# Moving the rounds of a top-k search on VectorE: the first token half's rounds go beside the indexer, the second half's go one to every two attention units

## The chip, the cores and the metric

The kernel runs on one core of one Trainium2 chip. The metric is the device time of one execution in microseconds (us), lower is better. The engines are named as in the profile: PE (TensorE matmul), PEld (its weight loads), DVE (VectorE), ACT (ScalarE), POOL (GpSimd), SP (the queue that issues the DMAs).

## The reference, cut to what matters

The program is one dense transformer block and then two layers of a second kind, for 256 tokens. Each of the two layers mixes tokens with two attentions of 8 heads, and one of them sees only keys that an indexer has chosen:

```python
n_keep = min(TOPK_MAX, T // 4)                     # 64 of 256 keys
rel = relu(einsum('bthd,bsd->bths', iqb, ik) * IDX_DIM ** -0.5)   # 8 indexer heads
score = einsum('bths,bth->bts', rel, iwb)
score = where(key_idx <= tq, score, -inf)
_, sel = top_k(score, n_keep)                      # the sparse attention (DSA) reads these keys
# the first attention (MLA) needs none of it
s = einsum('bthd,bshd->bhts', qb, k) * scale
p = softmax(where(key_idx <= tq, s, -inf))
```

Everything is float32. After the two attentions come an output projection, a layer norm, a router and 16 experts.

## The kernel before, in words

The kernel is one program in which every engine has its own instruction stream, written in the order in which it runs; semaphores join them. There is no scheduler. The 256 tokens are two halves of 128 (`half` 0 and 1); because of causality half 0 has 128 keys and half 1 has 256.

In each of the two layers these stages follow one another:

1. The indexer, 16 steps `i` (`half`, head): PE makes a score tile (L2347) between the matmuls of three projections (L2054 to L2056), ACT applies the relu into one of two `logit` buffers (L1018), DVE adds it, weighted, to `score` (`idx_add`, L1753 and L1756; the profile calls this tile `bias_h`). PE's tile of step i waits for relu i-2, relu i waits for add i-2, so the three run at most two steps apart. DVE also copies projection results out of PSUM (`save_half`, L1309) after steps 6, 10 and 14. POOL turns the queries by their positions meanwhile (`rotate`, L662 to L665).
2. The turning of q and k: PE transposes pairs of heads (L1979) into four banks used in turn. ACT copies q out (L1047), DVE copies k out (L1786, `k_t`). Group i of k is only written once the copy of group i-2 is done, and DVE's copies stand behind all 16 adds. Then PE makes sums for the router (L2385).
3. The first attention, 16 units (half, head): PE scores (L2133), DVE adds the mask and takes the row maximum (`logits`, L1279), ACT takes the exponential (`exps`, L839), PE transposes (L1979), ACT copies (L848) and casts a quarter slab of the next weights (L755), PE weighs the values (L2149). `attention` on DVE takes `before` and `after`, called around each unit's `logits`. After unit 12 DVE divides and saves the first half (`save(0)`, L1285 and L1288), at the end the second.
4. The sparse attention, whose `logits` first adds the selection to a bias (L1272).

The largest 64 keys of a row are found in 8 rounds for each half. A round is `largest(i)`, which takes the 8 largest (MAX, L1802), and `take(i)`, which overwrites them (MATCH_REPLACE, L1807, two instructions in the trace). `selection()` then turns what was taken into a mask (L1816, L1821). Before the change all 16 rounds stand in the first attention, one to a unit, round i around unit i.

Of the kernel before, what the change touches and what calls it, by code (L numbers as in the profile page):

```python
# [30 lines left out]
ALU = mybir.AluOpType  # L31
AX = mybir.AxisListType

P = 128
SEQ, D = 256, 1024
HALVES = SEQ // P
DC = D // P
HEADS, HD = 8, 64
WIDTH = HEADS * HD
EPS_RMS, EPS_LN = 1e-6, 1e-5  # L40
NEG = -1e30
# [15 lines left out]
IDX_HEADS, IDX_D = 8, 32  # L57
KEEP = SEQ // 4
# [22 lines left out]
SC_MLA = MLA_D ** -0.5  # L81
# [3 lines left out]
TAKEN = -3e38  # L85
# [14 lines left out]
L_IN, L_IN_B, L_IN_C, L_QUP, L_UK, L_UV, L_O = 0, 4, 6, 7, 9, 10, 11  # L100
# [144 lines left out]
def build(nc, A, out):  # L245

    ctx = ExitStack()
    with ctx:
        def sb(name, shape, dt=F32):
            return ctx.enter_context(nc.sbuf_tensor(name, shape, dt))  # L250

        S = {name: ctx.enter_context(nc.semaphore(name)) for name in SEMAPHORES}
        bank = [ctx.enter_context(nc.psum_tensor(f"bank{i}", [P, 512], F32)) for i in range(8)]
# [21 lines left out]
        value = sb("value", [P, HALVES, WIDTH])  # L275
# [3 lines left out]
        k_t = sb("k_t", [P, HEADS, SEQ])  # L279
# [38 lines left out]
        mask = const[:, C_MASK:C_DIST].rearrange("p (a t) -> p a t", a=HALVES)  # L318
        dist = const[:, C_DIST:C_COS1].rearrange("p (a t) -> p a t", a=HALVES)
        before, one = marks[:, 0:P], marks[:, P:P + 1]  # L320
# [21 lines left out]
        k_up = wide_b[:].rearrange("p (a h d) -> p a h d", a=HALVES, h=HEADS)  # L342
# [94 lines left out]
        def wait_slab(eng, name, n, j=None, per=0):  # L437

            eng.wait_ge(S[name], count(n + 1, j, per))
# [34 lines left out]
        IDX_AFTER_QUP, IDX_AFTER_UK, IDX_AFTER_UV = 6, 10, 14  # L474
        N_IDX = HALVES * IDX_HEADS
# [22 lines left out]
        def k_turned(i):  # L498
            return bank[3 - 2 * (i % 2)]
# [700 lines left out]
        def _(dve):  # L1200
            w = Waits(dve, S)
            split = [0]
            tt = nc.vector.tensor_tensor
# [102 lines left out]
            def save_half(n, name, saves):  # L1306
                wait_slab(dve, "slab_used", n)
                for dst, src in saves:
                    nc.vector.tensor_copy(dst, src).then_inc(S[name], 1)  # L1309
# [305 lines left out]
            for g in range(GROUPS):  # L1615
                nc.vector.scalar_tensor_tensor(
                    out=xs[:, 4 + g, SEQ:2 * SEQ], in0=bank[6 + g // 2][:, (g % 2) * SEQ:(g % 2 + 1) * SEQ],
                    scalar=vec[:, V_PS + g:V_PS + g + 1], in1=xs[:, 4 + g, 0:SEQ].bitcast(F32),
                    op0=ALU.mult, op1=ALU.subtract).then_inc(S["mixed_lo"], 1)
# [38 lines left out]
            for i in range(HALVES):  # L1658
# [7 lines left out]
                                               scalar=1.0 / D, in1=stat[:, 1, 4 + i:5 + i], op0=ALU.mult,  # L1666
                                               op1=ALU.add).then_inc(S["mean_square"], 1)
# [47 lines left out]
            for layer in range(LAYERS):  # L1715
                b = layer_base(layer)
# [27 lines left out]
                score = sel_score  # L1744

                def idx_add(i):
                    half, h = divmod(i, IDX_HEADS)
                    keys = P * (half + 1)
                    dst = score[:, half, 0:keys]
                    w.next("idx_relu")  # L1750
                    weight = idx_w[:, half, h:h + 1]
                    if h == 0:
                        nc.vector.tensor_scalar(dst, logit[:, i % 2, 0:keys], weight, None, ALU.mult)\  # L1753
                            .then_inc(S["idx_added"], 1)
                    else:
                        nc.vector.scalar_tensor_tensor(out=dst, in0=logit[:, i % 2, 0:keys], scalar=weight, in1=dst,  # L1756
                                                       op0=ALU.mult, op1=ALU.add).then_inc(S["idx_added"], 1)
                    w.next("idx_added")

                def save_qup(i):  # L1760
                    save_half(b + L_QUP + i, "qup_saved1",
                              [(q_up[:, 1, 4 * i:4 * i + 4, 0:MLA_D],
                                bank[QUP_BANKS[i] + 1][:, 0:4 * MLA_D].rearrange("p (h d) -> p h d", h=4))])
# [8 lines left out]
                turned_b(5)  # L1772
                splits_to(b + L_UV)
                w.next("idx_masked")
                for i in range(N_IDX):
                    idx_add(i)
                    if i + 1 == IDX_AFTER_QUP:
                        save_qup(1)
                    if i + 1 == IDX_AFTER_UK:
                        save_half(b + L_UK, "kv_saved1",  # L1780
                                  [(k_up[:, 1, :, 0:HD], bank[1][:].rearrange("p (h d) -> p h d", h=HEADS))])
                    if i + 1 == IDX_AFTER_UV:
                        save_half(b + L_UV, "kv_saved1", [(value[:, 1, :], bank[5][:])])
                for i in range(4):
                    w.next("turned_a", 2)
                    nc.vector.tensor_copy(k_t[:, 2 * i:2 * i + 2, :], k_turned(i)[:].rearrange("p (c t) -> p c t", c=2))\  # L1786
                        .then_inc(S["copied_k"], 1)
                for half in range(HALVES):
                    keys = P * (half + 1)
                    dst = score[:, half, 0:keys]  # L1790
                    tt(dst, dst, mask[:, half, 0:keys], ALU.add).then_inc(S["idx_masked"], 1)
                w.next("idx_masked", HALVES)

                assert KEEP // 8 == HEADS

                def largest(i):
                    half = i // HEADS
                    if i:  # L1800
                        w.next("vector_step")
                    nc.vector.max(best, score[:, half, 0:P * (half + 1)]).then_inc(S["vector_step"], 1)  # L1802

                def take(i):
                    dst = score[:, i // HEADS, 0:P * (i // HEADS + 1)]
                    w.next("vector_step")
                    nc.vector.match_replace(dst, best, dst, TAKEN).then_inc(S["vector_step"], 1)  # L1807

                def selection():

                    w.next("vector_step")
                    for half in range(HALVES):
                        keys = P * (half + 1)
                        dst = score[:, half, 0:keys]

                        nc.vector.tensor_scalar(dst, dst, TAKEN * 0.5, -NEG, ALU.is_le, ALU.mult).then_inc(S["vector_step"], 1)  # L1816
                    w.next("vector_step", HALVES)
                    for half in range(HALVES):
                        keys = P * (half + 1)
                        dst = score[:, half, 0:keys]  # L1820
                        nc.vector.scalar_tensor_tensor(out=dst, in0=dst, scalar=NEG, in1=mask[:, half, 0:keys],  # L1821
                                                       op0=ALU.add, op1=ALU.add).then_inc(S["vector_step"], 1)
                    w.next("vector_step", HALVES)

                attention(SC_MLA, 0, before=largest, after=take, at_end=selection)

                def heads_low(i):

# [872 lines left out]
```

## Time and profile before

| | us |
|---|---|
| median of 3 runs | 1126.9 (1126.75 to 1127.37) |
| the profiled execution | 1127.47 |
| its span, first to last instruction | 1125.7 |
| PE busy | 1076.1 (96%) |
| DVE busy | 563.8 (50%) |
| ACT busy | 436.8 (39%) |

The span holds two layers of the second kind; the indexer of the first begins near 428 us and its first attention near 447 us, those of the second near 801 and 820 us. DVE's 50% is a mean over stages: between 463 and 467 us it is nearly fully busy.

### The profile page before, as it was taken

The page shows a single profiled execution, that of the slowest core. Times are in us where ns is not written, and L with a number is a line of the kernel's source. Part 1 is how long each engine was busy: PE and PEld are TensorE (multiplying, and loading weights), DVE is VectorE, ACT ScalarE, POOL GpSimd, SP SyncE. Part 2 cuts the span into 40 slices and gives each one's busy share as a digit, 9 for nine tenths or more (in the row PEclk, how much of TensorE's full clock was granted, in tenths as well). Part 3 has the DMA queues.
Part 4 walks back from the last instruction along what each step waited for, and adds up shares of the span by engine and source line. Part 5 has one row for each costly group of instructions (what it writes and reads, how often), then busy time and mean ns, then how long its engine had stood idle before and what let it go on. Part 6 is the DMA issues. An engine that isn't in the chain of part 4 may idle for free.

```text
span 1125.7 us, 16190 instructions
## 1 busy us (share of the span) xinstructions
PE 1076.1 (96%) x6206; PEld 741.4 (66%) x6210; DVE 563.8 (50%) x1081; ACT 436.8 (39%) x797; POOL 90.0 (8%) x113
## 2 busy tenths in 40 slices
PE   8999998999999999899999999989989999999996
PEld 5898987999999788686444443348977744444332
DVE  4664376676676647846422222264685642232224
ACT  5445455554554435744211111144475422221111
POOL 1200000000000011520000000020242000000000
PEclk8999998999999999899999999989989999999998
DMA  7843245545655345428999999944542989999993
GB/s 273 269 145 130 89 150 185 179 162 189 202 166 189 128 147 184 152 98 357 411 420 422 419 422 422 419 176 151 187 144 82 376 355 422 420 421 420 422 420 144
DMA packets 82829, 294.60 MB, mean 262 GB/s; under 512 B 8424, under 2 KB 41542, under 8 KB 58058
## 3 DMA queue, kind: packets, MB, share of 16 engines
q1 hardware_dynamic: 79888, 289.33, 67.5%
q10 hardware_dynamic: 2874, 4.36, 1.0%
q8 instruction: 44, 0.72, 0.3%
q14 instruction: 23, 0.19, 0.0%
HBM read 292.62 MB, written 1.05 MB: 261 GB/s over the span
## 4 chain that ended last, share of the span: by engine, by line
PE 82%; DVE 6%; DMA 6%; ACT 3%; issue 2%; SPq 0%; DVEq 0%; POOL 0%; ACTq 0%
PE bank L2519 16%; PE bank L2528 9%; PE bank L2054 8%; PE bank L2055 8%; PE bank L2056 8%; DMA early_w<-in_w_up 5%; PE bank L2115 4%; PE bank L2117 4%; PE bank L2116 4%; PE bank L1979 4%; PE bank L2506 3%; PE bank L2149 3%; PE bank L2551 2%; PE bank L2133 2%; PE bank L2231 1%
## 5 line engine op out<-in xcount | busy, mean ns | idle before, releaser
L1208 DVE TENSOR_TENSOR lo<-raw,hi 128x2048 fp32r<-128x2048 f32 (+3 forms) x77 | 164.7, 2146 | 63.8 <-ACT hi L747 63.5
L747 ACT CAST hi<-raw 128x2048 fp32r<-128x2048 f32 (+3 forms) x78 | 139.5, 1795 | 60.9 <-PE bank L2056 58.6
L1454 DVE TENSOR_TENSOR proj<-bank,proj 64x512 f32<-64x512 f32 x32 | 34.7, 1083 | 210.0 <-PE bank L2541 209.9
L2115 PE MATMUL bank<-xs,hi 128*128 128x256 f32 x448 | 128.8, 287 | 3.1 <-DVE xs L1238 1.5
L2054 PE MATMUL bank<-hi,xs 128*128 128x512 f32 (+2 forms) x312 | 125.3, 402 | 6.6 <-DVE xs L1242 3.4
L2116 PE MATMUL bank<-xs,hi 128*128 128x256 f32 x448 | 127.7, 285 | 0.0
L2117 PE MATMUL bank<-xs,lo 128*128 128x256 f32 x448 | 127.7, 285 | 0.0
L2056 PE MATMUL bank<-lo,xs 128*128 128x512 f32 (+2 forms) x312 | 118.6, 380 | 0.0
L2055 PE MATMUL bank<-hi,xs 128*128 128x512 f32 (+2 forms) x312 | 118.5, 380 | 0.0
L1137 ACT ACTIVATE proj<-bank 64x512 f32<-64x512 f32 x32 | 18.9, 589 | 191.4 <-PE bank L2520 191.4
L2115 PEld LDWEIGHTS bank<-xs,hi 128*128 128x128 f32 x448 | 87.0, 194 | 4.6 <-issue 3.0
L2116 PEld LDWEIGHTS bank<-xs,hi 128*128 128x128 f32 x448 | 87.0, 194 | 0.4
L2117 PEld LDWEIGHTS bank<-xs,lo 128*128 128x128 f32 x448 | 86.9, 194 | 0.0
L2054 PEld LDWEIGHTS bank<-hi,xs 128*128 128x128 f32 x312 | 60.1, 193 | 16.8 <-DVE lo L1553 3.7
L2520 PE MATMUL bank<-moe_w,xg 128*64 128x512 f32 x160 | 70.3, 592 | 0.0
L1472 DVE SCALAR_TENSOR_TENSOR expert_out<-bank,slot_gate,expert_out 128x512 fp32r<-128x512 f32 x32 | 24.0, 751 | 88.8 <-ACT expert_out L1150 88.8
L2056 PEld LDWEIGHTS bank<-lo,xs 128*128 128x128 f32 x312 | 59.8, 192 | 10.7
L2055 PEld LDWEIGHTS bank<-hi,xs 128*128 128x128 f32 x312 | 60.2, 193 | 8.9
L1150 ACT ACTIVATE expert_out<-bank,slot_gate 128x512 fp32r<-128x512 f32 x32 | 22.0, 688 | 110.8 <-PE bank L2528 110.8
L1689 DVE SCALAR_TENSOR_TENSOR proj<-bank,conv,proj 128x255 f32<-128x255 f32 (+1 forms) x88 | 38.5, 478 | 48.7 <-ACT proj L967 45.8
L2528 PE MATMUL bank<-moe_w,act_t 128*64 128x512 f32 x256 | 59.8, 601 | 0.9 <-ACT act_t L1141 0.9
L643 POOL TENSOR_TENSOR stat<-stat,power 128x1 f32<-128x1 f32 (+2 forms) x15 | 16.5, 1098 | 499.6 <-DVE stat L1936 227.0
(292 smaller groups left out, 2206.5 us busy)
## 6 DMA issues: line engine op xcount, KB each, us to landing
raw<-in_w_up SPq DMA_DIRECT2D x34, 1024.0 KB, 5.1
moe_w<-in_w_down SPq DMA_DIRECT2D x32, 1024.0 KB, 19.4
raw<-in_w_in SPq DMA_DIRECT2D x28, 1024.0 KB, 5.4
moe_w<-in_w_up SPq DMA_DIRECT2D x20, 1024.0 KB, 20.9
raw<-in_w_down SPq DMA_DIRECT2D x19, 1024.0 KB, 5.3
early_w<-in_w_gate SPq DMA_DIRECT2D x12, 1024.0 KB, 18.7
early_w<-in_w_up SPq DMA_DIRECT2D x12, 1024.0 KB, 20.8
raw<-in_w_gate SPq DMA_DIRECT2D x10, 1024.0 KB, 16.2
```

Of the source, the lines that this page charges most:

```text
L747: nc.scalar.copy(high(n)[:, 0:size], raw[:, n % RING, 0:size]).then_inc(S["hi_done"], 1)
L1208: tt(low(n)[:, 0:size], raw[:, n % RING, 0:size], high(n)[:, 0:size].bitcast(F32), ALU.subtract).then_inc(S["lo_done"], 1)
L1979: return nc.tensor.transpose(dst, src, ident[0:src.shape[0], 0:src.shape[0]])
L2054: mm(out_, lhs_hi, rhs_hi, start=first, stop=False)
L2055: mm(out_, lhs_lo, rhs_hi, start=False, stop=False)
L2056: return mm(out_, lhs_hi, rhs_lo, start=False, stop=last)
L2115: mm(dst, wh[:, k, col], x_hi, start=k == 0, stop=False)
L2116: mm(dst, wh[:, k, col], x_lo, start=False, stop=False)
L2117: ins = mm(dst, wl[:, k, col], x_hi, start=False, stop=k == k_chunks - 1)
L2519: mm(to[0:SLOTS, :], rows_[:, kk, :], gate[:, k, :], start=kk == 0, stop=kk == DC - 1)
L2520: ins = mm(to[SLOTS:P, :], rows_[:, kk, :], up[:, k, :], start=kk == 0, stop=kk == DC - 1)
L2528: ins = mm(to[SLOTS * c:SLOTS * (c + 1), :], act[:, kk, :], down[:, k, 512 * c:512 * (c + 1)], start=kk == 0, stop=kk == 3)
```

## The change

Only DVE's stream changes; the streams of PE, ACT, POOL and SP are the same rows in the same order. The causal mask of half 0 is added right after indexer step 8 (when that half's scores are complete) instead of behind the k copies. Rounds 0 to 6 of half 0 stand in indexer steps 9 to 15: `largest` ahead of the step's add, `take` behind it. Round 7 stands at the head of the first attention. Half 1's eight rounds stand around the odd units 1, 3, ..., 15. The mask of half 0 is made at unit 2, that of half 1 at the end.

```diff
                 for i in range(N_IDX):
+                    if i > IDX_HEADS:
+                        largest(i - IDX_HEADS - 1)
                     idx_add(i)
+                    if i == IDX_HEADS:
+                        causal(0)
+                    if i > IDX_HEADS:
+                        take(i - IDX_HEADS - 1)
                     if i + 1 == IDX_AFTER_QUP:
                         save_qup(1)
...
-                for half in range(HALVES):
-                    keys = P * (half + 1)
-                    dst = score[:, half, 0:keys]
-                    tt(dst, dst, mask[:, half, 0:keys], ALU.add).then_inc(S["idx_masked"], 1)
-                w.next("idx_masked", HALVES)
...
+                causal(1)
+
+                def ranked_beside(i):
+
+                    if i == 0:
+                        largest(HEADS - 1)
+                        take(HEADS - 1)
+                    elif i % 2:
+                        largest(HEADS + i // 2)
+                    elif i == 2:
+                        selected(0)
+
+                def taken_beside(i):
+
+                    if i % 2:
+                        take(HEADS + i // 2)
...
-                attention(SC_MLA, 0, before=largest, after=take, at_end=selection)
+                attention(SC_MLA, 0, before=ranked_beside, after=taken_beside, at_end=selection)
```

`causal(half)` is the masking that stood in the removed loop, `selected(half)` the two instructions of the old `selection()` for one half; `largest` and `take` are unchanged.

On DVE, from indexer step 8 to the first k copy, before (`bias_h` is the score, `wide_b` and `value` are results that DVE saves for others):

```order
L1753 TENSOR_SCALAR bias_h<-logit,idx_w 128x256
L1756 SCALAR_TENSOR_TENSOR bias_h<-logit,idx_w,bias_h 128x256
L1309 COPY wide_b<-bank 128x8x64
L1756 SCALAR_TENSOR_TENSOR bias_h<-logit,idx_w,bias_h 128x256 x4
L1309 COPY value<-bank 128x512
L1756 SCALAR_TENSOR_TENSOR bias_h<-logit,idx_w,bias_h 128x256 x2
L1786 COPY k_t<-bank 128x512 x4
```

The same place after the change, from step 8 to step 11 (steps 12 to 15 repeat the last three rows, with the copy of `value` behind step 13's):

```order
L1753 TENSOR_SCALAR bias_h<-logit,idx_w 128x256
L1780 TENSOR_TENSOR bias_h<-bias_h,const 128x128
L1787 MAX power<-bias_h 128x8
L1756 SCALAR_TENSOR_TENSOR bias_h<-logit,idx_w,bias_h 128x256
L1792 MATCH_REPLACE bias_h<-power,bias_h 128x128
L1309 COPY wide_b<-bank 128x8x64
L1787 MAX power<-bias_h 128x8
L1756 SCALAR_TENSOR_TENSOR bias_h<-logit,idx_w,bias_h 128x256
L1792 MATCH_REPLACE bias_h<-power,bias_h 128x128
L1787 MAX power<-bias_h 128x8
L1756 SCALAR_TENSOR_TENSOR bias_h<-logit,idx_w,bias_h 128x256
L1792 MATCH_REPLACE bias_h<-power,bias_h 128x128
```

One masking, seven MAX and seven MATCH_REPLACE now stand ahead of the k copies, which PE's transposes wait for.

On DVE, in the first attention around `save(0)`, between units 12 and 13, before:

```order
L1807 MATCH_REPLACE bias_h<-power,bias_h 128x256
L1285 RECIPROCAL row_inv<-row_sum 128x8
L1288 TENSOR_TENSOR xn<-bank,row_inv 128x512
L1802 MAX power<-bias_h 128x8
L1279 ISA logit,row_min<-bank,const 128x256
```

The same place after the change:

```order
L1279 ISA logit,row_min<-bank,const 128x256
L1279 ISA row_min 128x1
L1285 RECIPROCAL row_inv<-row_sum 128x8
L1288 TENSOR_TENSOR xn<-bank,row_inv 128x512
L1787 MAX power<-bias_h 128x8
L1279 ISA logit,row_min<-bank,const 128x256
```

The MATCH_REPLACE of unit 12 is gone from ahead of the saving, since even units have no round.

## Rows read from the trace of the kernel before

**Rows 1.** The page: busy time of each engine, and the chain's shares by engine.

```profile
PE 1076.1 (96%) x6206; PEld 741.4 (66%) x6210; DVE 563.8 (50%) x1081; ACT 436.8 (39%) x797; POOL 90.0 (8%) x113
...
PE 82%; DVE 6%; DMA 6%; ACT 3%; issue 2%; SPq 0%; DVEq 0%; POOL 0%; ACTq 0%
```

**Rows 2.** The chain that ended last, indexer's tail (start us, us, what), last two: layer 1.

```profile
441.43 0.50 DVE bias_h L1756
...
443.59 0.70 DVE k_t L1786
444.34 1.53 PE bank L1979 x12
445.87 1.72 PE bank L2385 x16
...
816.39 0.70 DVE k_t L1786
...
822.11 0.29 DVE power L1802
```

**Rows 3.** Timeline of DVE, indexer and k copies of layer 0 (start, duration, idle before).

```profile
434.56 0.81 DVE L1756 SCALAR_TENSOR_TENSOR bias_h<-logit,idx_w,bias_h 128x128 f32<-128x128 f32 x1 [0.64 <-ACT logit L1018]
435.80 0.35 DVE L1753 TENSOR_SCALAR bias_h<-logit,idx_w 128x256 f32<-128x256 f32 x1 [0.42 <-ACT logit L1018]
436.92 0.92 DVE L1756 SCALAR_TENSOR_TENSOR bias_h<-logit,idx_w,bias_h 128x256 f32<-128x256 f32 x1 [0.77 <-ACT logit L1018]
437.88 0.69 DVE L1309 COPY wide_b<-bank 128x512 f32<-128x512 f32 x1
438.48 0.48 DVE L1756 SCALAR_TENSOR_TENSOR bias_h<-logit,idx_w,bias_h 128x256 f32<-128x256 f32 x1
...
440.31 0.48 DVE L1756 SCALAR_TENSOR_TENSOR bias_h<-logit,idx_w,bias_h 128x256 f32<-128x256 f32 x1 [0.65 <-ACT logit L1018]
...
442.56 0.99 DVE L1756 SCALAR_TENSOR_TENSOR bias_h<-logit,idx_w,bias_h 128x256 f32<-128x256 f32 x2
...
446.51 0.62 DVE L1791 TENSOR_TENSOR bias_h<-bias_h,const 128x128 f32<-128x128 f32 x2
```

**Rows 4.** Timeline of DVE in the first attention of layer 0, three places.

```profile
448.13 0.09 DVE L1807 MATCH_VALUE_LOAD bias_h<-power,bias_h 128x8 f32 x1
448.20 0.28 DVE L1807 MATCH_REPLACE8 bias_h<-power,bias_h 128x128 f32<-128x128 f32 x1
448.51 0.30 DVE L1802 MAX8 power<-bias_h 128x8 f32<-128x128 f32 x1
448.73 0.27 DVE L1279 CUSTOM_DVE_ANT_0 logit<-bank,const 128x128 f32<-128x128 f32 x1
...
463.07 0.41 DVE L1807 MATCH_REPLACE8 bias_h<-power,bias_h 128x256 f32<-128x256 f32 x1
463.40 0.20 DVE L1285 RECIPROCAL row_inv<-row_sum 128x8 f32<-128x8 f32 x1
...
470.70 0.69 DVE L1288 TENSOR_TENSOR xn<-bank,row_inv 128x512 f32<-128x512 f32 x1 [1.19 <-PE bank L2149]
```

**Rows 5.** Timeline of POOL in layer 0's indexer: the rotation's first group.

```profile
433.80 2.95 POOL L662 TENSOR_TENSOR gates<-wide_a,const 128x256 f32<-128x256 f32 x4 [12.06 <-DVE wide_a L1309]
```

**Rows 6.** Timeline of ACT in the first attention, exponentials of units 13 and 14.

```profile
465.02 0.51 ACT L839 ACTIVATE prob<-logit,row_min 128x256 f32<-128x256 f32 x1 [0.53 <-DVE row_min L1279]
...
466.30 0.51 ACT L839 ACTIVATE prob<-logit,row_min 128x256 f32<-128x256 f32 x1
```

**Rows 7.** Windows: stretch, its length, busy us (x) of PE, PEld, DVE, ACT, POOL, granted clock.

```profile
449.00:450.00 1.00, 0.36 (x2) 0.36 (x3) 0.84 (x7) 0.96 (x5) 0.00 (x0) 0.80 0.88 225
450.00:452.00 2.00, 1.85 (x9) 1.45 (x9) 1.41 (x10) 1.29 (x6) 0.00 (x0) 0.50 0.97 363
...
461.00:463.00 2.00, 1.68 (x12) 1.28 (x11) 1.89 (x7) 2.00 (x8) 1.15 (x1) 1.00 0.00 0
```

**Rows 8.** Timeline of PE: eight transposes at the half clock, in layer 0.

```profile
419.91 1.91 PE L1979 MATMUL bank<-const,proj 128*128 128x128 f32 x8
```

More of the change, by code:

```diff
@@ L1774, in _, with causal, largest, take @@
                 w.next("idx_masked")
+                assert KEEP // 8 == HEADS
+                def causal(half):
+                    dst = score[:, half, 0:P * (half + 1)]
+                    tt(dst, dst, mask[:, half, 0:P * (half + 1)], ALU.add).then_inc(S["idx_masked"], 1)
+                    w.next("idx_masked")
+                def largest(i):
+                    half = i // HEADS
+                    if i:
+                        w.next("vector_step")
+                    nc.vector.max(best, score[:, half, 0:P * (half + 1)]).then_inc(S["vector_step"], 1)
+                def take(i):
+                    dst = score[:, i // HEADS, 0:P * (i // HEADS + 1)]
+                    w.next("vector_step")
+                    nc.vector.match_replace(dst, best, dst, TAKEN).then_inc(S["vector_step"], 1)
+                def selected(half):
+                    dst = score[:, half, 0:P * (half + 1)]
+                    w.next("vector_step")
+                    nc.vector.tensor_scalar(dst, dst, TAKEN * 0.5, -NEG, ALU.is_le, ALU.mult).then_inc(S["vector_step"], 1)
+                    w.next("vector_step")
+                    nc.vector.scalar_tensor_tensor(out=dst, in0=dst, scalar=NEG, in1=mask[:, half, 0:P * (half + 1)],
+                                                   op0=ALU.add, op1=ALU.add).then_inc(S["vector_step"], 1)
                 for i in range(N_IDX):
+                    if i > IDX_HEADS:
+                        largest(i - IDX_HEADS - 1)
                     idx_add(i)
+                    if i == IDX_HEADS:
+                        causal(0)
+                    if i > IDX_HEADS:
+                        take(i - IDX_HEADS - 1)
                     if i + 1 == IDX_AFTER_QUP:
@@ L1787, in _ @@
                         .then_inc(S["copied_k"], 1)
-                for half in range(HALVES):
-                    keys = P * (half + 1)
-                    dst = score[:, half, 0:keys]
-                    tt(dst, dst, mask[:, half, 0:keys], ALU.add).then_inc(S["idx_masked"], 1)
-                w.next("idx_masked", HALVES)
[L1796 to L1802, printed above, removed]
@@ L1804, in take @@
-                def take(i):
-                    dst = score[:, i // HEADS, 0:P * (i // HEADS + 1)]
-                    w.next("vector_step")
[L1807 to L1823, printed above, removed]
@@ L1827, in heads_low, with selection @@
+                def selection():
+                    selected(1)
+                    w.next("vector_step")
+                attention(SC_MLA, 0, before=ranked_beside, after=taken_beside, at_end=selection)
                 def heads_low(i):
```

## The prediction

> **What bounds the kernel now.** I read the page first. PE is busy 96% of the span and has 82% of the chain that ended last, DVE 6% [rows 1]. A change to DVE alone can matter only where DVE stands in that chain. So I read the chain in the stages the change touches, then the timelines of DVE, ACT, PE and POOL there.
>
> Two places count, in each layer. The first is the indexer's tail. From step 13 on the chain runs through DVE: the adds and a copy, then the first k copy at 443.59, behind which PE's last 12 transposes start at 444.34, and behind those PE's sums [rows 2]. Nothing there is slack: an instruction put on DVE ahead of the k copies moves 444.34 by its full price. Layer 1 has the same k copy in the chain at 816.39 [rows 2].
>
> The second place is the first attention. DVE looks nearly full in it (1.89 of 2.00 us from 461 to 463) [rows 7], but ACT is full (2.00 of 2.00) [rows 7]. Before that, from 450 to 460, PE has the half clock, 1.2 GHz (granted 0.50), and little idle time (1.85 busy of 2.00 in the sample) [rows 7]. So DVE's rounds there are mostly beside an engine that is full anyway. The one clear stall that DVE causes is at unit 13, where ACT waits 0.53 us for it [rows 6], because `save(0)` stands between units 12 and 13. In layer 1 one MAX (0.29) is on the chain near the start [rows 2].
>
> **The change, part by part.**
>
> *Prices on DVE, start to start.* MAX of 128 keys to the next independent instruction: 448.51 to 448.73, 0.22. The load of the match values ahead of MATCH_REPLACE: 448.13 to 448.20, 0.07. MATCH_REPLACE to a MAX that needs its result: 448.20 to 448.51, 0.31 [rows 4]. An add with 256 keys to one that needs it: 0.51, as 442.56 to 443.59 holds two [rows 2, 3]. A copy of 512: 437.88 to 438.48, 0.60 [rows 3].
>
> *One indexer step of half 1 with a round in it:* 0.22 + 0.51 + 0.07 + 0.31 = 1.11 us. Data arrive every 1.12 us (adds at 440.31 and 441.43, both waiting on ACT about 0.65) [rows 2, 3]. So a plain step just fits, and nothing is ever made up: what DVE once falls behind stays.
>
> *What it falls behind by, layer 0.* The first add of half 1 starts at 435.80 and is done at 436.15 [rows 3]. The masking of 128 keys, 0.31 (two, one of them longer, take 0.62 [rows 3]), ends near 436.48, then MAX. Step 9's add starts with its data at 436.92, and takes 0.92 as before [rows 3], done at 437.86. Then 0.07, MATCH_REPLACE at 437.94, the copy of `wide_b` 0.23 later at 438.17 (an independent instruction follows after about what it does behind a MAX, 0.22), and the next MAX at 438.78. The copy costs 0.53 beyond a plain step, since the MATCH_REPLACE drains beneath it. From there four plain steps and the copy of `value`, 4 x 1.11 + 0.53 = 4.97, bring the MAX of step 14 to 443.75, one more that of step 15 to 444.86. Its add, match load and MATCH_REPLACE take 0.22 + 0.51 + 0.07 + 0.23 = 1.03, and the first k copy starts at 445.9. Before it was 443.59: **2.3 us late**, and PE's transposes with it. PE keeps waiting; the copies, transposes and sums behind keep their order and spacing. DVE's masking of half 1 and round 7 behind the last k copy (0.35 + 0.35 + 0.07 + 0.23, about 1.0) replace two maskings and a MAX (446.51 to about 447.4 [rows 3]) and are beneath PE's 1.72 us of sums [rows 2]: nothing.
>
> *Bounds of this term.* Below: if step 9's add took 0.48, as the others do, the term is 2.3 - 0.44 = 1.9. Above: both slow adds (0.81 where 0.35 is usual, 0.92 where 0.48 is) lie beside POOL's rotation, which runs on behind its first group [rows 3, 5]. If the masking too has to wait out a POOL instruction, 2.95 / 4 = 0.74, of which 0.22 is free (a MAX at 436.48 lets step 9's add go at 436.70, its data come at 436.92), it is 2.3 + 0.5 = 2.8. I take 2.3 for both layers.
>
> The Trainium skill (SBUF — State Buffer, "SBUF: two separate sides") says that GpSimd and VectorE share a port pair under an exclusive lock, which a VectorE instruction with two SBUF inputs takes and others do not. By that rule the masking at 436.15 (two SBUF inputs) would be held until POOL's instruction ends, MAX and MATCH_REPLACE never, and the sum would sit between 2.3 and 2.8. The two slow adds agree with it.
>
> *What the attention gives back.* At unit 13 the MATCH_REPLACE of unit 12 no longer stands ahead of `save(0)`: 463.07 to 463.40 = 0.33 of the 0.53 us stall [rows 4, 6]. The MAX of unit 13 still stands there. In layer 1's start, where a MAX of 0.29 is on the chain, fewer rounds give 0.25 or so; in layer 0 the clock has fallen by then, PE is the bound, and I take nothing. The selection at the end is two instructions shorter on DVE, but `save(1)` waits there 1.19 us for PE [rows 4], so nothing. Lower bound 0; upper bound the whole stall and a whole MAX, 0.53 + 0.29 = 0.8 a layer. I take 0.3 in layer 0 and 0.6 in layer 1.
>
> *Sum.* Layer 0: +2.3 - 0.3 = +2.0. Layer 1: +2.3 - 0.6 = +1.7. Together +3.7 us. Everything behind the attention is released by it, the loads of the experts' weights too, so I let the delay pass through whole. The profiled execution would go from 1127.47 to 1131.2; it lies 0.57 above the median, so the median goes from 1126.9 to **1130.6**. The bounds of the terms give 2 x (1.9 - 0.8) = 2.2 and 2 x 2.8 = 5.6, so 1129.1 to 1132.5.
>
> **The rivals.**
>
> *The clock falls in the tail.* PE now idles at full clock for 2.3 us between transposes. In layer 0 the clock fell within 449 to 450 (0.80 in that microsecond, 0.50 behind it), when PE was busy 0.36 of 1.00 [rows 7], so a gap of 2.3 us may well do it. The clock would then be half for the 12 transposes and 16 sums: eight transposes take 1.91 at half clock [rows 8] and 12 take 1.53 at full [rows 2], so about +1.2 for 12, and the sums at most double, +1.7. That is +2.9 a layer, part of it given back because the attention's slow stretch could end sooner. One layer: 1133.5; both: up to 1136.4. Against it: ahead of that fall PE had small matmuls and the attention's first waits; here transposes, gap-free but for this one gap, stand on both sides. The Trainium skill (TensorE: Matmul & The Clock Gate, "What's actually happening") describes a gate that follows recent activity and is either at 1.2 or 2.4 GHz. The windows show both levels and nothing between over a whole stretch; by that rule the rival is possible, and each layer decides it anew.
>
> *The rounds are hidden.* DVE idles 0.65 and 0.77 us ahead of two adds of half 1 [rows 3], the round's own 0.60 us fits a step, and the two copies could be absorbed if PE and ACT slip along. Then only the gain stays: 1126.9 - 0.9 = 1126.0. Against it: the adds at 438.48 and 442.56 come with no idle time at all [rows 3], and seven rounds with the masking add 7 x 0.60 + 0.31 = 4.5 us to a stretch whose idle time is 0.42 + 0.77 and at most three times 0.65, 3.1.
>
> *Faster.* DVE was the pace of the attention's second half after all: it is busy 1.89 of 2.00 us [rows 7]. With half the rounds a unit could drop from its 1.28 us (465.02 to 466.30 [rows 6]) by, as an estimate, a quarter of a MAX, 0.08, as ACT's own work is about that close behind: 7 x 0.08 = 0.6, and with the stall's 0.53 1.1 a layer. It decides only if the tail's delay is under 1.1 us, that is if five of seven rounds are hidden. With no delay it gives 1124.7. ACT's 2.00 of 2.00 speaks against.
>
> *A smaller loss.* The tail is late as worked out, but some wait behind the attention, for experts' weights (DMA has 6% of the chain [rows 1]), takes up half of it: 1128.7.
>
> **How the numbers follow.** Forecast 0.60 (1129.1 to 1132.5). Clock in the tail 0.20. Smaller loss 0.09. Hidden 0.07. Faster 0.04. The range keeps the forecast, most of the smaller loss and one layer's clock: 1128.3 to 1134.5. A change of 0.2%, 2.3 us, is about the least that a measurement of this kernel can tell from none, so "slower" begins at 1129.2. Slower: 0.60 less its lowest edge, and the clock's 0.20, and a little of the smaller loss, 0.83. Same: 0.12. Faster: 0.05.
>
> **What the changed profile would show.** Right: no idle time on DVE ahead of the adds of steps 10 to 15; the first k copy near 445.9; PE idle 2.3 us more between its transposes, waiting on DVE's `k_t`; ACT's wait at unit 13 down to 0.2; the first scores near 449.7. Wrong: a k copy before 445, or idle DVE between rounds (hidden); a granted clock of 0.50 during PE's sums (clock); units of half 1 closer than 1.28 us (faster); the sparse attention less than 3 us late in layer 1 though the tail was (smaller loss). What would make me wrong most simply is the 1.11 against 1.12: each tenth that a step costs more adds 0.6 us a layer, while no saving shows below 1.12.

## The result and the profile after

The changed kernel takes 1131.83 us (median of 7 runs, 1130.99 to 1141.68), the kernel before beside it on the same chip 1126.9 (7 runs, 1123.08 to 1129.69). The ratio is 1.0059, 95% interval 1.0035 to 1.0083: slower, by 4.9 us between the medians and by some 6.6 by the ratio. The forecast was 1130.6 with a range of 1128.3 to 1134.5. The profiled execution of the change took 1131.23, that of before 1127.47: +3.76, where the sum in the prediction said +3.7. Both have the same mean granted clock, 0.973, so these two can be laid beside each other stretch by stretch.

The page of the changed kernel, busy time of each engine and the chain's shares, against [rows 1]:

```profile
PE 1076.5 (95%) x6210; PEld 742.1 (66%) x6210; DVE 564.4 (50%) x1081; ACT 435.5 (39%) x797; POOL 90.0 (8%) x113
...
PE 80%; DVE 8%; DMA 6%; ACT 3%; issue 3%; SPq 0%; DVEq 0%; POOL 0%; ACTq 0%
```

DVE's work has grown by 0.6 us and PE's by 0.4, but two points of the chain went from PE to DVE. No sum of busy time says so; only the chain does. The chain of the changed kernel in the indexer's tail of layer 0 (start us, us, what), against [rows 2]:

```profile
434.06 0.36 DVE bias_h L1753
...
434.45 0.72 DVE bias_h L1780
...
435.19 0.29 DVE power L1787
...
436.49 0.60 DVE wide_b L1309
...
444.04 0.61 DVE k_t L1820
...
444.70 1.53 PE bank L1998 x12
446.23 1.71 PE bank L2404 x16
```

From the end of the indexer's first half onward every piece of the chain is DVE's, masking, MAX, add, replace and copy in turn, until PE takes over at 444.70. Before, that began only at step 13. The transposes and sums behind have kept their lengths, 1.53 and 1.71. DVE's own timeline there, against [rows 3]:

```profile
434.45 0.71 DVE L1780 TENSOR_TENSOR bias_h<-bias_h,const 128x128 f32<-128x128 f32 x1
...
435.40 0.70 DVE L1756 SCALAR_TENSOR_TENSOR bias_h<-logit,idx_w,bias_h 128x256 f32<-128x256 f32 x1
...
436.21 0.28 DVE L1792 MATCH_REPLACE8 bias_h<-power,bias_h 128x128 f32<-128x128 f32 x1
436.41 0.68 DVE L1309 COPY wide_b<-bank 128x512 f32<-128x512 f32 x1
437.01 0.28 DVE L1787 MAX8 power<-bias_h 128x8 f32<-128x128 f32 x1
...
438.10 0.29 DVE L1787 MAX8 power<-bias_h 128x8 f32<-128x128 f32 x1
438.31 0.47 DVE L1756 SCALAR_TENSOR_TENSOR bias_h<-logit,idx_w,bias_h 128x256 f32<-128x256 f32 x1
438.81 0.09 DVE L1792 MATCH_VALUE_LOAD bias_h<-power,bias_h 128x8 f32 x1
438.89 0.27 DVE L1792 MATCH_REPLACE8 bias_h<-power,bias_h 128x128 f32<-128x128 f32 x1
439.20 0.29 DVE L1787 MAX8 power<-bias_h 128x8 f32<-128x128 f32 x1
...
440.30 0.29 DVE L1787 MAX8 power<-bias_h 128x8 f32<-128x128 f32 x1
...
441.88 0.28 DVE L1787 MAX8 power<-bias_h 128x8 f32<-128x128 f32 x1
...
443.96 1.28 DVE L1820 COPY k_t<-bank 128x512 f32<-128x512 f32 x2
```

No row has an idle time in brackets, and none of the rows left out between them has one: the waits for ACT of [rows 3] (0.77, 0.65) are gone from step 9 on. A plain step takes 1.10 us from MAX to MAX, one with a copy in it 1.58 (440.30 to 441.88). And PE's timeline at the same place:

```profile
444.70 0.65 PE L1998 MATMUL bank<-const,wide_b 128*128 128x128 f32 x4 [2.05 <-DVE k_t L1820]
```

PE stands idle for 2.05 us and names DVE's `k_t` as what it waited for. The exponentials of units 12 to 14 on ACT in layer 0's attention, against [rows 6]:

```profile
462.77 0.51 ACT L839 ACTIVATE prob<-logit,row_min 128x256 f32<-128x256 f32 x1
...
463.53 0.62 ACT L755 CAST hi<-raw 128x512 fp32r<-128x512 f32 x1
464.28 0.51 ACT L839 ACTIVATE prob<-logit,row_min 128x256 f32<-128x256 f32 x1
...
465.56 0.51 ACT L839 ACTIVATE prob<-logit,row_min 128x256 f32<-128x256 f32 x1
```

Unit 12's row of before, which [rows 6] lack, is this:

```profile
463.12 0.51 ACT L839 ACTIVATE prob<-logit,row_min 128x256 f32<-128x256 f32 x1
```

Before, unit 13 came 1.90 us behind unit 12 (463.12 to 465.02), now it comes 1.51 us behind; the next one takes 1.28 in both. So 0.39 us of the stall is gone, and ACT's idle time ahead of unit 13 is down from 0.53 us to 0.13 (464.15, where the cast ends, to 464.28). The windows against [rows 7] (length, busy us of PE, PEld, DVE, ACT, POOL, granted clock):

```profile
449.00:450.00 1.00, 0.12 (x2) 0.00 (x0) 0.93 (x6) 0.99 (x4) 0.00 (x0) 1.00 1.10 238
450.00:452.00 2.00, 1.59 (x8) 1.38 (x9) 1.33 (x8) 1.52 (x8) 0.00 (x0) 0.76 0.97 287
...
461.00:463.00 2.00, 1.88 (x13) 1.63 (x14) 1.29 (x8) 2.00 (x7) 1.36 (x2) 1.00 0.00 0
```

In the attention's second half DVE has dropped from 1.89 to 1.29 of 2.00 us and ACT is still at 2.00: ACT, not DVE, was the pace there.

**Where the time went.** The table cuts the two profiled executions at five events that both have in each layer: the first add with 256 keys (step 8), the first k copy, the attention's first scores, the sparse attention's first scores, the first row of the router. Each row is the time between two events, in us.

| stretch | before, layer 0 / 1 | after, layer 0 / 1 | difference |
|---|---|---|---|
| start to step 8 (layer 0 only) | 435.80 | 434.06 | -1.74 |
| step 8 to first k copy | 7.79 / 7.79 | 9.90 / 9.89 | +2.11 / +2.10 |
| first k copy to scores | 3.82 / 3.82 | 3.81 / 3.81 | 0.0 |
| first attention | 23.02 / 22.22 | 21.92 / 21.78 | -1.10 / -0.44 |
| sparse attention to router | 47.87 / 47.88 | 48.86 / 48.39 | +0.99 / +0.51 |
| router of layer 0 to step 8 of layer 1 | 290.30 | 291.70 | +1.40 |
| router of layer 1 to the end | 235.39 | 235.28 | -0.11 |

The row that the change was costed on, +2.1 twice, is the whole of what DVE's stream can explain in the tail. The first row lies ahead of any edited instruction (half clock for 17.1 us in it before and for 10.2 after), and most of the rest, positive and negative, is the granted clock: PE ran at half clock for 10.2 us in the first attention of layer 0 before and for 6.8 after, in the sparse attention behind it for 3.4 and then 6.8, and between the router and the next indexer for 10.2 and then 13.6 (summed from windows of one microsecond). That these cancel to leave +3.7 is partly luck, and the experiments had to show how much.

### The profile page after: what moved, and what is told of

Read it like the earlier page. It is cut to its first block, busy times and chain, and to the rows that moved or that the text cites. A ratio compares the mean times of both kernels' runs of the same rounds, so it can differ in the third digit from the quotient of the medians.

```text
span 1129.4 us, 16194 instructions
## 1 busy us (share of the span) xinstructions
PE 1076.5 (95%) x6210; PEld 742.1 (66%) x6210; DVE 564.4 (50%) x1081; ACT 435.5 (39%) x797; POOL 90.0 (8%) x113
## 4 chain that ended last, share of the span: by engine, by line
PE 80%; DVE 8%; DMA 6%; ACT 3%; issue 3%; SPq 0%; DVEq 0%; POOL 0%; ACTq 0%
PE bank L2538 16%; PE bank L2547 9%; PE bank L2073 8%; PE bank L2075 7%; PE bank L2074 7%; DMA early_w<-in_w_up 5%; PE bank L2134 4%; PE bank L2136 4%; PE bank L2135 4%; PE bank L1998 3%; PE bank L2525 3%; PE bank L2168 2%; PE bank L2570 2%; PE bank L2152 2%; PE bank L2250 1%
```

## The experiments

The kernels ran in two groups, the first beside 16 runs of the kernel before (median 1126.95), the second beside 29 (1127.22). Since one profile of a kernel holds another sample of clock stretches than the next, each is read in three ways: its median, the length of the stretches above, and the time of all its runs put at one mean clock. For the last, 119 runs of nine kernels (all but the first seven of the kernel before, whose clocks are not on record) were fitted with one slope, which is 0.66 us (standard error 0.05) for each 0.001 of the mean granted clock, and one level for each kernel. That column leaves out what a kernel loses by lowering its own clock, so it is to be read beside the median and not in its place.

| kernel | median (range, runs) | ratio, 95% | mean clock | against before at equal clock | step 8 to scores |
|---|---|---|---|---|---|
| before | 1126.95 and 1127.22 (45) | 1 | 0.9744 | 0 | 11.61 / 11.61 |
| the change | 1131.83 and 1134.12 (13) | 1.0059, 1.0073 | 0.9707 | +4.2 ± 0.4 | 13.71 / 13.70 |
| only the early rounds | 1137.29 (1133.96 to 1139.92, 4) | 1.0089, 1.0065 to 1.0114 | 0.9670 | +5.1 ± 0.8 | 13.71 / 16.28 |
| only the spread | 1131.93 (1128.66 to 1134.19, 5) | 1.0053, 1.0035 to 1.0072 | 0.9700 | +1.6 ± 0.6 | 11.61 / 11.60 |
| three rounds early | 1131.70 (1125.92 to 1135.39, 10) | 1.0032, 1.0011 to 1.0053 | 0.9715 | +2.1 ± 0.5 | 11.60 / 11.60 |
| a delay alone | 1135.52 (1133.49 to 1138.33, 6) | 1.0078, 1.0061 to 1.0096 | 0.9698 | +5.7 ± 0.6 | 15.39 / 13.92 |
| change, PE's gap filled | 1131.71 (1128.54 to 1134.41, 12) | 1.0039, 1.0027 to 1.0051 | 0.9732 | +3.6 ± 0.4 | 13.70 / 13.71 |
| before, k copies on ACT | 1127.37 (1124.95 to 1131.19, 12) | 1.0003, 0.9989 to 1.0017 | 0.9726 | -0.7 ± 0.4 | 11.32 / 11.32 |
| three early, k on ACT | 1129.01 (1127.11 to 1130.66, 12) | 1.0013, 1.0002 to 1.0025 | 0.9711 | -0.5 ± 0.5 | 11.32 / 11.32 |

("±" is one standard error of the fit; in the last column layer 0 and layer 1 of the profiled execution.)

**The change once more, on the chip of the first group.** No edit.

> The changed kernel once more, as a control for what a single profile is worth. Theory (VectorE's work ahead of the k copies): from the first add of indexer steps 8 to 15 to the first k copy 9.9 us in both layers, as in the first profile of it (before: 7.8), whatever the clock does; first score to first sparse score between 21.8 and 23.0. Rival (what was lost is the clock's luck): the stretches from the sparse attention to the router and the whole time differ from the first profile by more than 1 us, while the indexer's stretch doesn't.

1134.12 us (1129.83 to 1139.52, 6 runs), ratio 1.0073 (1.0046 to 1.0100). Step 8 to k copy is 9.89 in both layers and its profiled span 1129.2, within 0.2 of the first profile of the change (1129.4). What varies between its runs is the clock: the run at a mean clock of 0.975 took 1129.83, that at 0.969 1135.55. So the loss has a fixed part and one that each execution draws anew.

**Only the early rounds.** Half 0's rounds stay beside the indexer, half 1's go back to one per unit.

```diff
-                    elif i % 2:
-                        largest(HEADS + i // 2)
-                    elif i == 2:
-                        selected(0)
+                    elif i >= HEADS:
+                        largest(i)
...
-                    if i % 2:
-                        take(HEADS + i // 2)
+                    if i >= HEADS:
+                        take(i)
```

> Only the first part: rounds 0 to 6 of half 0 stay in the indexer and round 7 at unit 0, but half 1's eight rounds stand one to a unit in units 8 to 15 as before, and both selections at the end. Theory: the indexer's stretch is 9.9 us as in the full change, and ACT waits again 0.5 us at unit 13, since the MATCH_REPLACE is back ahead of the saving: time at or 0.3 to 0.9 us above the full change, 3 to 5 above before. Rival (spreading half 1 costs, the indexer doesn't): time at before's.

1137.29 us, 10.3 above before, where 3 to 5 were expected; at equal clock it is 5.1 ± 0.8, and the rest is clock (0.9670, four runs). Step 8 to k copy is 9.90 in both layers, as in the change: the tail's delay belongs to this part. ACT's wait at unit 13 is back at 0.52 us, since unit 12 again has a round. In layer 0, where both have 6.8 us of half clock in the first attention, it takes 22.35 us against the change's 21.92: 0.43 us is what the wider spacing of half 1 gives in these two profiles. In layer 1 this execution also shows the rival "the clock falls in the tail". Its windows there, and PE's timeline:

```profile
823.00:824.00 1.00, 0.04 (x1) 0.00 (x0) 0.97 (x4) 0.59 (x1) 0.00 (x0) 1.00 0.00 0
824.00:825.00 1.00, 0.00 (x0) 0.00 (x0) 0.97 (x5) 0.00 (x0) 0.00 (x0) 1.00 0.00 0
825.00:826.00 1.00, 0.91 (x6) 0.91 (x7) 0.64 (x3) 0.00 (x0) 0.00 (x0) 0.70 0.00 0
826.00:828.00 2.00, 2.00 (x12) 2.00 (x10) 0.99 (x2) 0.59 (x1) 0.00 (x0) 0.50 0.00 0
```

```profile
825.09 0.86 PE L1997 MATMUL bank<-const,wide_b 128*128 128x128 f32 x4 [2.05 <-DVE k_t L1820]
825.75 1.06 PE L1997 MATMUL bank<-const,wide_a 128*128 128x128 f32 x4
826.60 1.06 PE L1997 MATMUL bank<-const,wide_b 128*128 128x128 f32 x4
827.45 3.46 PE L2403 MATMUL bank<-router_gb,const 128*128 128x32 f32 x16
```

PE does nothing for two microseconds, goes on at full clock at 825.09, and the clock falls some 0.3 us later (0.70 in that microsecond). Four transposes then take 1.06 us for 0.60, sixteen sums 3.46 for 1.87, and the scores come 6.38 us behind the first k copy instead of 3.82: +2.56, where the rival had +2.9 (its +1.2 for the transposes is +1.0, its +1.7 for the sums +1.6). The clock stays down for 17.1 us, far into the attention, which takes 22.74 us against layer 0's 22.35. In layer 0 of the same execution, with the same gap, the clock held. The Trainium skill (TensorE: Matmul & The Clock Gate, "What's actually happening") has the clock follow recent activity between these two levels. The rows agree in the levels and in the order, idle first and the fall behind it; the page by itself would not tell layer 0 from layer 1.

**Only the spread.** The early rounds are taken out of the indexer. Half 0's eight stand around units 0 to 7, half 1's around the odd units as in the change, so the odd ones of units 0 to 7 hold two. The masking of half 0 goes back behind the k copies.

```diff
-                    if i > IDX_HEADS:
-                        largest(i - IDX_HEADS - 1)
                     idx_add(i)
...
-                    if i == 0:
-                        largest(HEADS - 1)
-                        take(HEADS - 1)
+                    if i < HEADS:
+                        largest(i)
...
+                    if i < HEADS:
+                        take(i)
+                        if i % 2:
+                            largest(HEADS + i // 2)
+                            take(HEADS + i // 2)
```

> Only the second part: no round in the indexer, half 0's rounds in units 0 to 7 as before, half 1's eight rounds one to every odd unit on top. Theory: the indexer's stretch is back at 7.8 us. A pair of units 0 to 7 then holds three rounds on VectorE, about 0.95 + 1.7 us, against 2.1 to 2.3 us that TensorE needs at half clock, so the first half gets 0.3 to 0.5 us a pair longer, 1.2 to 2 us a layer, less the stall at unit 13: 1 to 3 us above before. Rival (VectorE has room there): at or below before.

1131.93 us, 5.0 above before, where 1 to 3 were expected. The tail is as before (7.79 and 7.78 to the k copy), but the first attention takes 23.97 and 23.87 us against 23.02 and 22.22. The exponentials of units 2 and 6 of its layer 0 show where:

```profile
448.44 0.40 ACT L839 ACTIVATE prob<-logit,row_min 128x128 f32<-128x128 f32 x1 [0.84 <-DVE row_min L1279]
...
453.57 0.40 ACT L839 ACTIVATE prob<-logit,row_min 128x128 f32<-128x128 f32 x1 [0.34 <-DVE row_min L1279]
```

Behind the doubled rounds of units 1 and 5 ACT waits for DVE, 0.84 and 0.34 us, which it did neither before nor in the change, and unit 8's exponential comes 11.52 us after the first scores, against 10.24 before and 10.10 in the change. So half 1's wider spacing in this form, with half 0's rounds left where they were, gives nothing. Two thirds of this median's distance from before is the clock (0.9700): at equal clock it is +1.6. The two attentions are 2.6 longer than before's, but layer 1's has 10.2 us of half clock in it where before's had 6.8. Against before's layer 0, which has 10.2 too, they are 0.95 and 0.85 longer, together 1.8.

**Three rounds early.** Only rounds 0 to 2 of half 0 stay beside the indexer; the other thirteen are spread over units 0 to 11 and 14, never at 12 and 13.

```diff
+                EARLY = 3
...
-                    if i > IDX_HEADS:
+                    if 0 <= i - IDX_HEADS - 1 < EARLY:
                         largest(i - IDX_HEADS - 1)
...
+                ROUND_AT = {0: 3, 1: 4, 2: 5, 3: 6, 4: 7, 5: 8, 6: 9, 7: 10, 8: 11, 9: 12, 10: 13, 11: 14, 14: 15}
...
+                    if i in ROUND_AT:
+                        largest(ROUND_AT[i])
```

> A smaller dose: only rounds 0 to 2 stand in the indexer (steps 9 to 11); rounds 3 to 15 stand at units 0 to 11 and 14 of the first attention, so that units 12 and 13, around the saving, have none. Theory (backlog): by the steps' prices VectorE has caught up by step 13, so the first k copy comes 7.8 to 8.0 us after step 8's add, as before, not 9.9; ACT's wait at unit 13 falls to nothing: time 0 to 2 us below before. Rival (every round in the indexer costs its own share of the 2.1 us, 0.3 each): 8.7 us, time 0 to 1 us above before.

The tail did what the backlog says. DVE's timeline in layer 0:

```profile
440.75 0.28 DVE L1792 MATCH_REPLACE8 bias_h<-power,bias_h 128x128 f32<-128x128 f32 x1
440.94 1.10 DVE L1756 SCALAR_TENSOR_TENSOR bias_h<-logit,idx_w,bias_h 128x256 f32<-128x256 f32 x2
442.08 0.69 DVE L1309 COPY value<-bank 128x512 f32<-128x512 f32 x1
442.68 0.99 DVE L1756 SCALAR_TENSOR_TENSOR bias_h<-logit,idx_w,bias_h 128x256 f32<-128x256 f32 x2
443.71 1.29 DVE L1821 COPY k_t<-bank 128x512 f32<-128x512 f32 x2
```

The k copy stands 7.78 us behind step 8, as in the kernel before: the steps without a round (0.5 us each) catch up what the masking and three rounds had put off. Three rounds cost nothing there, seven cost 2.1 us. The first attention takes 22.47 and 22.54, and ACT has no wait left at unit 13. Yet the median is 1131.7, +2.1 at equal clock, not below before. The profiled execution (1135.39, mean clock 0.966) shows one reason. Its window behind the layer norm of layer 1, and PE's timeline in the first dense matmuls:

```profile
753.00:760.00 7.00, 6.42 (x18) 4.82 (x19) 6.54 (x6) 3.59 (x5) 2.23 (x3) 0.52 0.11 13
```

```profile
759.13 0.63 PE L2075 MATMUL bank<-lo,xs 128*128 128x512 f32 x1
759.55 0.63 PE L2073 MATMUL bank<-hi,xs 128*128 128x512 f32 x1
...
760.29 0.39 PE L2075 MATMUL bank<-lo,xs 128*128 128x512 f32 x1
```

Here the half clock lies on matmuls that are PE-bound, 0.43 us apart instead of 0.23, and costs 2.7 us (the lag behind the change's profile goes from 1.0 to 3.7 between 752 and 760, where the two profiles reach the same matmul). In the change's profile it had fallen near 745, on matmuls of zeros (L2189, there to keep PE busy) and in before's too, where it cost next to nothing. So a mean clock says how long PE was slow, not what it was doing then. Whether this kernel's other slow executions have the same stretch, and why its mean clock is lower than before's (0.9715 against 0.9744), is not shown.

**A delay alone.** The kernel before, with five dependent MAX of 256 keys ahead of the k copies; their results are not used.

```diff
+                for _ in range(5):
+                    nc.vector.max(best, score[:, 1, :]).then_inc(S["vector_step"], 1)
+                    w.next("vector_step")
                 for i in range(4):
                     w.next("turned_a", 2)
                     nc.vector.tensor_copy(k_t[:, 2 * i:2 * i + 2, :], k_turned(i)[:]
```

> The kernel before with nothing moved; five extra MAX instructions of 256 keys on VectorE (their result is never used) stand ahead of the first k copy, 2.1 to 2.3 us of VectorE work in each layer. Theory (what costs is VectorE's lateness at the k copies, and the clock that TensorE's idle time can cost): first k copy 9.9 to 10.1 us after step 8's add, first attention as before or shorter by its clock; time 4 to 9 us above before, at or above the full change (which gets 0.3 to 0.6 us a layer back). Rival (the cost is in the moved rounds, the late adds or relus or the attention's new order): 4 us less than the full change at least in the attention's part, time within 2 us of before.

```profile
443.80 2.28 DVE L1785 MAX8 power<-bias_h 128x8 f32<-128x256 f32 x5
446.11 1.29 DVE L1789 COPY k_t<-bank 128x512 f32<-128x512 f32 x2
```

The k copy comes 10.10 us behind step 8, +2.31. In layer 0 the clock fell at the end of PE's gap, here 2.38 us long (granted 0.63 from 446 to 448, 0.52 in the next two) and k copy to scores takes 5.29 us; in layer 1 it held, 3.81. The median is 8.3 us up, for 4.6 us of delay: in this kernel the gap costs more than its length, and some 3 us of it are its lower clock (0.9698). At equal clock it is 5.7 ± 0.6, so nothing behind the tail takes up a delay. That this is more than 4.6 is within two standard errors and shows nothing further.

**The change with PE's gap filled.** Nine matmuls of zeros, which the kernel has for such places, run on PE in the gap.

```diff
+                        if i == 2 and src is k_up:
+                            pe.wait_ge(S["idx_relu"], N_IDX * layer + 15)
+                            busy(9, bank[6])
```

> The changed kernel with nine matmuls of 512 columns of zeros on TensorE (their result is never used) in the gap between its transposes, about 2 us. Theory (2.1 us a layer lost for good, and beyond that the clock falls in some executions after the gap): the k copy is as late as in the change, 9.9 us after step 8's add, k copy to first score 3.8 us in every profile, the mean granted clock over the executions is at or above 0.972 against 0.971 of the change, and the mean time drops by 1 to 3 us towards 1131. Rival (the clock has nothing to do with the gap): mean time and clock as for the change, about 1133.8 and 0.971.

```profile
442.30 0.66 PE L1998 MATMUL bank<-const,wide_a 128*128 128x128 f32 x4
443.00 1.91 PE L2189 MATMUL bank<-zeros 128*128 128x512 bf16 x8
445.00 0.66 PE L1998 MATMUL bank<-const,wide_b 128*128 128x128 f32 x4
```

The delay is all there (9.89 in both layers) and the gap is busy. The mean clock rises from the change's 0.9707 to 0.9732 (the difference has a standard error of 0.0012) and the mean time falls from 1133.8 to 1131.5 us, by 2.3 ± 1.1, in 13 and 12 runs. These are two standard errors, and the change did not run beside the filled kernel: it is what one would see if PE's idling cost some 2 us in clock, and not proof of it. What remains is 4.3 us over the kernel before, 3.6 ± 0.4 at equal clock; the delay of 4.2 less what the two attentions give back is about 3.3.

**Before, with the k copies on ACT.** The four copies move from DVE's stream to ACT's, between the q copies.

```diff
-                    w.skip("turned_a")
+                    w.next("turned_a")
+                    nc.scalar.copy(k_t[:, 2 * i:2 * i + 2, :], k_turned(i)[:].rearrange("p (c t) -> p c t", c=2))\
+                        .then_inc(S["copied_k"], 1)
```

> The kernel before, with the four k copies on ACT instead of VectorE. Theory (the k copies behind the adds are what joins VectorE to the path): TensorE's seventh and eighth group of transposes no longer wait for VectorE, first score 11.1 to 11.6 us after step 8's add against 11.6: time 0 to 1 us below before, not to be told from it. Rival (ACT becomes late with eight copies of about 0.5 us): first score later than 11.8 us, time 0.5 to 2 us above before.

```profile
441.21 0.59 ACT L1047 COPY q_t<-bank 128x512 f32<-128x512 f32 x1
441.69 0.60 ACT L1050 COPY k_t<-bank 128x512 f32<-128x512 f32 x1
```

ACT carries all eight copies without a gap, and the scores come 11.32 us behind step 8 instead of 11.61. That is 0.3 us a layer, and the whole kernel is the same as before (1.0003, 0.9989 to 1.0017).

**Three early, with the k copies on ACT.** DVE now has room behind its adds while PE turns q and k: rounds 3 to 7 of half 0 and its mask go there, half 1's eight are spread over units 1 to 14.

```diff
+                for i in range(3, HEADS):
+                    largest(i)
+                    take(i)
+                selected(0)
                 causal(1)
+                ROUND_AT = {1: 8, 3: 9, 5: 10, 7: 11, 8: 12, 10: 13, 11: 14, 14: 15}
```

> Candidate from the theory: rounds 0 to 2 of half 0 in indexer steps 9 to 11, where VectorE idled; the four k copies on ACT; rounds 3 to 7 and the mask of half 0 on VectorE beside TensorE's transposes and sums; half 1's eight rounds at units 1, 3, 5, 7, 8, 10, 11 and 14. Theory: first score 11.1 to 11.8 us after step 8's add, no wait of ACT for VectorE at unit 13, first score to first sparse score 0.5 to 1 us shorter than before at the same clock: 1 to 3 us below before, 5 to 8 below the change. Rival (VectorE's five rounds in a row come too late for unit 0, or the clock's luck rules): at before's time or 1 to 4 above it, as three_early was.

1129.01 us: about 4.9 us (by the means) better than the change, and not better than before but 0.1% slower (ratio 1.0013, 1.0002 to 1.0025). The five rounds end at 445.4, one microsecond ahead of unit 0's instruction on DVE (446.4), and the scores come 11.32 us behind step 8; the first attention takes 22.33 and 21.58 us, the least sum of any kernel here with undelayed scores. But 49.79 and 48.81 us follow to the router where before had 47.87 and 47.88, and the mean clock is 0.9711. At equal clock it is level with before, -0.5 ± 0.5. The expected gain of 1 to 3 us was not there.

## Why the prediction was right, point by point

**What bounds the tail: right.** That nothing is slack ahead of the k copies was read from [rows 2]. A delay alone, with no round moved, passed through whole; with the k copies on another engine, five rounds at the same place did not delay the scores (11.32 us behind step 8 with them and without).

**The backlog, 2.3 us a layer: right in mechanism, 0.2 too long, 2.11 and 2.10 measured.** Against the prediction's steps, all counted from step 8's add: the copy of `wide_b` at 2.35 (forecast 2.37), the next MAX at 2.95 (2.98), that of step 14 at 7.82 (7.95), that of step 15 at 8.92 (9.06), the k copy at 9.90 (10.1). A plain step is 1.10, not 1.11; a copy costs 0.48 beyond it, not 0.53; the last part is 0.98, not 1.03.

**POOL in the way: it came, and cost no more than the one slow add already in the sum.** The masking took 0.71 us where 0.31 was put, and step 9's add 0.70 where 0.92 was. POOL's timeline beside them:

```profile
432.06 2.95 POOL L662 TENSOR_TENSOR gates<-wide_a,const 128x256 f32<-128x256 f32 x4 [12.04 <-DVE wide_a L1309]
435.09 0.73 POOL L664 TENSOR_TENSOR wide_a<-gates 128x256 f32<-128x256 f32 x1
```

The masking (434.45) and the add (435.40) each end within 0.3 us of the end of a POOL instruction, and the MAX between them, with one SBUF input, takes its usual 0.29 beside POOL. That is the rule of the Trainium skill (SBUF — State Buffer, "SBUF: two separate sides"), and the trace agrees with it. The section names VectorE instructions in a 2-port performance mode beside those with two SBUF inputs; the prediction left them out with its "others do not", and nothing in its sum hangs on them. What the prediction drew from the rule, a sum between 2.3 and 2.8, did not come: it is 2.1. I had the masking's wait as 0 or 0.5 us. But it makes step 9's add begin later and so wait less for the next POOL instruction; both together end at 2.05 us, where the forecast, with a free masking and a slow add, had 2.06.

**What the attention gives back: the stall right, the total off by the clock.** ACT's idle time at unit 13 is 0.13 us, forecast 0.2; the stall is 0.39 shorter where 0.33 was put. In layer 1 the attention is 0.44 shorter (forecast 0.6), which the stall nearly accounts for: the 0.25 put down for the attention's start is not to be seen (unit 8's exponential comes 10.06 us behind the first scores, before 9.59). In layer 0 it is 1.10 shorter (0.3): the half clock began about 1.4 us later (0.76 from 450 to 452, against 0.50) and was 3.4 us shorter.

**Passing through whole: right in the sum, not place by place.** The prediction said nothing of the sparse attention (+1.0 and +0.5) nor of the experts (+1.4), nor of the start (-1.7), where nothing was edited. How far the stretch from the router of layer 0 to the next indexer moves with the clock can be read over the ten profiles, if it is cut where the dense matmuls of layer 1 begin. Ahead of them it is 234.5 to 235.2 us in nine profiles, whether 0, 1.0 or 6.8 us of it is at half clock (236.4 with 10.2 in only the early rounds). From there to the indexer's first add it is 48.0 us with no half clock (only the spread), 49.1 with 3.4 us (before, a delay alone), 50.6 to 50.7 with 6.8 (the change twice, only the early rounds, the filled gap, k copies on ACT, the last kernel) and 53.4 with 12.7 (three rounds early). So the change's +1.4 is the 3.4 us more of half clock on dense matmuls (+1.6 there, -0.2 ahead of it), about 0.4 us for each us of half clock; profiles with as much of it agree within 0.1 us whatever the kernel, so none of it is shown to come from the edit.

**The rivals.** "Hidden" and "faster" fell: no idle DVE between rounds, a k copy at 443.96 after a step 8 that came 1.74 us earlier, ACT still full with DVE at 1.29 of 2.00. "A smaller loss" fell too: at equal clock the change is 4.2 ± 0.4 us slower, beside the sum of 3.7, and the sparse attention of layer 1 begins 3.3 us later (842.43 before, 845.73 after). "The clock falls in the tail" is real, but belongs to executions and not to the kernel. It stood in two of the eight tails with a bare gap of some 2 us that were profiled (two layers each of the change twice, only the early rounds, a delay alone), and cost 2.56 and 1.48 us there. It should have been a part of the mean instead of an alternative to the forecast: the clock adds 2.4 us (0.0037 less of mean clock, at 0.66 us for 0.001) to the fixed 4.2, which makes the 6.6 by which the means of all runs differ (1133.8 and 1127.2). The tail's own falls account for about 1.0 of that 2.4, as an estimate: two in eight, some 2 us each, in two layers. Where the rest is lost is not shown. So the forecast's 1130.6 is near the medians' 1131.8 because it has the delay right; a mean loss of 6.6 us lies outside its sum, and the second set's median, 1134.12, is close to the range's upper edge.

**Open.** Why three rounds early and its relative on ACT, with tail and attention no longer than before's, do not beat it: at equal clock the one is 2.1 us slower, the other level. The sparse attention behind is 0.5 to 1.9 us longer in each of them. Part of this goes with the clock: over the twenty sparse attentions of the ten profiles, those with 3.4 us of half clock in them take 47.8 to 48.4 us, those with 6.8 us take 48.7 to 49.9, and three of these four have 6.8. Layer 0's 49.6 and 49.8 are still 0.7 to 0.9 above most others with 6.8 (48.7 to 48.9), and no wait of DVE or ACT in it was isolated; nor is it shown why their executions have a lower clock.

## What to carry to other kernels

An engine's idle time between data is room only if a step's own time with the added work stays under the spacing of its data: here 1.10 us of work against 1.12 leaves nothing to catch up with, so every first delay and every copy in the stretch reaches what is queued behind. Add up the backlog to the end of the stretch before moving work into it, look at what the in-order engine does next and who waits for that, and put in only as many steps as the remaining bare ones can catch up (here three, not seven). And weigh a new gap on PE above its length (here 8.3 us for 4.6 us of delay), count the clock as a part of the mean, and compare kernels by stretches and at equal clock: a profile that matches to 0.1 us can do so by cancelling.

## What the runs showed of the hardware

- A TensorE gap of 2.05 or 2.38 us came with a fall to the half clock in two of eight profiled places, and of the two layers of one execution only in one. With the gap filled by matmuls of zeros the mean granted clock was 0.9732 against 0.9707, two standard errors apart.
- One slope fits the runs of nine kernels: 0.66 us for 0.001 of mean clock. 6.8 us at half clock cost 2.7 us on PE-bound matmuls (48.0 to 50.7 us for one stretch, six profiles against one) and next to nothing on filler matmuls.
- Beside POOL, DVE's add of two SBUF tiles with 128 keys took 0.71 us for 0.31 or less alone, and an add with 256 keys 0.70 for 0.47; MAX and MATCH_REPLACE kept their times.
- An independent instruction starts 0.20 us behind a MATCH_REPLACE of 128 keys (436.21 to 436.41 by the timeline), a dependent one 0.31 behind.
